# Where the split weights and the activations start in on-chip memory: weights at 256 past a multiple of 512 bytes, activations at multiples of 512

## What is computed

```
layer 0: h += attention(rmsnorm(h))      # 8 heads over 9 chunks of 64 frames, 8 heads over 2 chunks
         h += (silu(n @ w_gate) * (n @ w_up)) @ w_down        # n = rmsnorm(h), inner width 2816
layer 1: h += (u * spatial_mix(rmsnorm(v))) @ w_out           # u, v = gelu(n @ w_in)
         h += top-2-of-8 experts, each a gate/up/down network  # inner width 3584
out = rmsnorm(h)
```

## Time and profile before

| | us |
|---|---|
| median of three executions | 3757.09 |
| lowest, highest | 3750.78, 3783.22 |
| the profiled execution, its own time | 3749.22 |
| its span, first to last instruction | 3747.5 |
| PE busy | 3575.2 (95%) |
| PEld busy | 3458.3 (92%) |
| DVE busy | 1760.1 (47%) |
| ACT busy | 1660.6 (44%) |
| mean granted TensorE clock | 0.981 of full speed |

### The profile page before, as it was taken

How to read it: one execution, slowest core, us unless ns; L and a number is a source line. 1 busy time by engine, 2 the same in 40 slices (tenths; PEclk the granted TensorE clock), 3 DMA queues, 4 the chain that set the end, 5 groups by cost and what they waited for, 6 DMA issues and landing times.

```text
span 3747.5 us, 76188 instructions
## 1 busy us (share of the span) xinstructions
PE 3575.2 (95%) x29176; PEld 3458.3 (92%) x29176; DVE 1760.1 (47%) x2508; ACT 1660.6 (44%) x2316; POOL 106.9 (3%) x137
## 2 busy tenths in 40 slices
PE   8999899999999999959999999999999999999993
PEld 5888799999999899659999999999999999999993
DVE  4455543333333544435555555554554444544444
ACT  3455433323332332236465564554654544544542
POOL 1000000000000000020000000000000000000001
PEclk9999999999999999979999999999999999999997
DMA  5111322333333422176666666556564455554446
GB/s 178 35 49 43 131 95 90 95 93 121 96 95 96 134 63 69 40 187 194 209 194 196 206 193 210 182 188 201 190 206 155 164 178 165 166 177 159 158 154 236
DMA packets 154482, 542.59 MB, mean 145 GB/s; under 512 B 18312, under 2 KB 18352, under 8 KB 154368
## 3 DMA queue, kind: packets, MB, share of 16 engines
q1 hardware_dynamic: 128592, 468.25, 39.2%
q0 software_dynamic: 16496, 55.52, 4.2%
q10 hardware_dynamic: 9280, 17.24, 1.6%
HBM read 511.31 MB, written 33.28 MB: 145 GB/s over the span
## 4 chain that ended last, share of the span: by engine, by line
PE 93%; DVE 2%; DMA 2%; ACT 1%; issue 1%; POOL 0%; ACTq 0%; POOLq 0%; DVEq 0%
PE ps L292 87%; PE ps L341 1%; PE ps L580 1%; PE ps L565 1%; PE ps L519 1%; DMA y<-yrow_d,slot 1%; PE ps L1524 1%; PE ps L1553 0%; PE ps L588 0%; PE ps L600 0%; DMA tok_d<-tokid,slot 0%; PE ps L1320 0%; PE ps L543 0%; ACT eA L639 0%; DVE wl L279 0%
## 5 line engine op out<-in xcount | busy, mean ns | idle before, releaser
L279 DVE TENSOR_TENSOR wl<-wraw,wh 128x1024 fp32r<-128x1024 f32 x876 | 1072.1, 1225 | 1462.1 <-ACT wh L275 1461.9
L275 ACT ACTIVATE wh<-wraw 128x1024 fp32r<-128x1024 f32 x876 | 921.4, 1058 | 1023.6 <-PE ps L292 1014.9
L292 PE MATMUL ps<-exh,wh 128*128 128x240 f32 (+3 forms) x3584 | 1021.0, 285 | 12.5 <-issue 10.1
L292 PE MATMUL ps<-exl,wh 128*128 128x240 f32 (+3 forms) x3584 | 1020.2, 285 | 0.0
L292 PE MATMUL ps<-exh,wl 128*128 128x240 f32 (+3 forms) x3584 | 1019.9, 285 | 0.0
L292 PE MATMUL ps<-xs,wh 128*128 128x256 f32 x5248 | 828.1, 280 | 3.1 <-DVE qAl L626 2.0
L292 PEld LDWEIGHTS ps<-xs,wh 128*128 128x128 f32 x5248 | 703.9, 189 | 11.6 <-issue 7.6
L292 PEld LDWEIGHTS ps<-exh,wh 128*128 128x128 f32 x3584 | 678.5, 189 | 13.4 <-issue 13.4
L292 PEld LDWEIGHTS ps<-exl,wh 128*128 128x128 f32 x3584 | 676.6, 189 | 0.0
L292 PEld LDWEIGHTS ps<-exh,wl 128*128 128x128 f32 x3584 | 676.6, 189 | 0.0
L292 PE MATMUL ps<-xs,wl 128*128 128x256 f32 x2624 | 518.1, 279 | 0.0
(11 more groups left out here) (280 smaller groups left out, 2802.6 us busy)
## 6 DMA issues: line engine op xcount, KB each, us to landing
wraw<-in_w_expert SPq DMA_DIRECT2D x676, 512.0 KB, 3.6
wraw<-in_w_main SPq DMA_DIRECT2D x200, 512.0 KB, 3.6
yrow_d<-yst ACTq DMA_DIRECT2D x16, 512.0 KB
yT<-in_xT POOLq DMA_DIRECT2D x4, 1024.0 KB, 10.3
hT<-in_xT POOLq DMA_DIRECT2D x2, 2048.0 KB, 10.0
h_d<-hT POOLq DMA_DIRECT2D x2, 2048.0 KB, 10.0
hT<-h_d POOLq DMA_DIRECT2D x2, 2048.0 KB, 13.6
xrow_d<-rows ACTq DMA_DIRECT2D x16, 256.0 KB, 2.0
```

The source lines that it names most:

```text
L275: act.activation(wh[:, j], wraw[:, j], ACT.Copy).then_inc(hi_done, 1)
L279: dve.tensor_tensor(wl[:, j], wraw[:, j], wh[:, j].bitcast(F32), ALU.subtract).then_inc(lo_done, 1)
L292: mm = pe.matmul(out[:, s], a, b[:, s], start=first and part == 0 and c == 0, stop=last and part == 2 and c + w == n)
```

## The change

No instruction, loop, semaphore or DMA is added, taken away or moved: on each of the five engines the order of instructions is the same. Only tensors are declared in another order. `gains` goes ahead of the weights and pushes them up by 128 bytes. `itab`, `nitem` and `upto` go to the end of the layout, behind `acc`, where they lie over nothing that is in use with them. A 64-byte tensor that nobody reads, `to_512`, fills the place before the activations.

```diff
+        gains = sb("gains", [P, 4, KD])
         wraw = sb("wraw", [P, 4, 1024])
         wh = sb("wh", [P, 4, 1024], F32R)
         wl = sb("wl", [P, 4, 1024], F32R)
         ident = sb("ident", [P, P])
         ones = sb("ones", [P, P])
-        gains = sb("gains", [P, 4, KD])
         epsc = sb("epsc", [P, 1])
...
         tokl = sb("tokl", [P, CAP // P], U32)
-        itab = sb("itab", [1, 3, NCAND + 1], I32)
-        nitem = sb("nitem", [1, 1], I32)
-        upto = sb("upto", [1, len(WIDTHS) + 1], I32)
+        sb("to_512", [P, 16])
...
         acc = sb("acc", [P, HALF], F32, s2)
+        itab = sb("itab", [1, 3, NCAND + 1], I32, s2)
+        nitem = sb("nitem", [1, 1], I32, s2)
+        upto = sb("upto", [1, len(WIDTHS) + 1], I32, s2)
         s2.close()
```

## The result

The changed kernel took 3795.58 us, the median of four executions (3794.92 to 3797.17). Beside it the kernel before took 3757.99, also of four (3750.78 to 3783.22). The ratio on record is 1.009 (that of the two medians is 1.010), with a 95% interval of 1.005 to 1.0129: slower by about one per cent. The profiled execution took 3797.17 us, its span is 3795.6, which is 48.1 us more than before. In the changed file `product`'s matmuls are line L293, and every later line is one further down.

A forecast was written before the change was run, and what follows sets the result against it. PE was taken to bound the kernel, through the three matmuls of `product` (L292). All terms were taken as 0 on the profiled 3749.2 us; with the median at 3757.1, the forecast was 3753 us, range 3630 to 3870.

The forecast's parts named there:

- weights and activations 256 apart instead of 192: Some 26,100 matmuls of L292, in the dense network and experts: new operand distance forecast to cost 0 us.
- best end: L292's products: all that is paid above the bound goes, together 196 us less, 3553 us left.
- worst end: L292's products: every one pays the value projections' 19.5 ns above its streaming time, 237 us more, 3986 us.
- the 109 ns: Pace of weight loads, read from twelve transposes of L1553 in 1.31 us; the bound for 240 and 256 columns.
- DVE, ACT and the transposes: Weight splitting covered by at least 2.7 us of PE work a unit, transposes at the weight-load pace; 0 us.
- The three transfers on the chain: DMA writes to moved tensors, 35.8 us on the chain; a tenth either way is 4 us, taken as 0.
- the lock: Phase of two streams at their start: 256-column matmuls share two paces anew, -31 to +32 us, taken as 0.
- A: L292's products: addresses count for nothing, or the change misses what matters; 3753 us, from 3715 to 3787; chance 0.44.
- B: L292's products: half of 512 bytes apart is better; 3651 us, from 3553 to 3715; chance 0.34.
- C: Experts and dense network: slower, excess half way between 192 and 320 apart; 118 us more, 3867 us; chance 0.22.
- the likeliest case: Whole kernel: addresses count for nothing, own range 3715 to 3787 us; chance 0.44.

The follow-up runs named there:

- its two twins: Two other layouts at distance 0 modulo 256: one pad of 64 bytes before the activations, or both operands starting at 320; 3800.14 and 3797.1 us.

## Why the prediction was wrong

**The step that failed** is the one on "weights and activations 256 apart instead of 192": "I take 0, since the only variation that the trace shows in one and the same product happens with no address changed". The distance decides the pace of these products. At a distance of 0 modulo 256 the 256-column matmuls cost 4.6 ns more than the mean of before. With the weights left where they were and the activations moved by one pad of 64 bytes to that distance, the loss is the same (`same_apart_256`).

**Why the reason given was none.** I argued that the pieces of a unit walk through all starts modulo 4096 and the pace does not move. They walk in steps of 512, and the activations in steps of 1024, 1536 or 2048. All of these are multiples of 256, the period that the runs showed. The trace of before had one distance in it, 192 modulo 256, for activations moving. It could not speak about another. Constancy over the variations that happen to be in a trace was taken for constancy over all.

**What was right.** The best end and worst end held: no product left them. Something is paid above the 109 ns and the columns' time, and it is the product's own. DVE, ACT and the transposes cost nothing more, as taken. The three transfers on the chain took 35.1 us instead of 35.8, which one trace of each cannot tell from chance. The facts behind the lock were read rightly: at the distance 192 two paces stand side by side with 256 columns (and two or three at 32, 128, 160 and 208), each trace changes between them only across a break in the stream, and which of them is taken changes from kernel to kernel. That a phase of the two streams "certainly" sets it is more than any run showed. The two paces fit the spread of the kernel before: its executions lie up to 30 us apart (3739.93 to 3769.97 in one set of 19), about the 31 or 32 us that I gave the lock either way. The four of the changed kernel, with one pace, lie within 2.3. But its two twins, with the same pace, spread over 9 and 10 us, and only the profiled executions show their paces, so this is an argument.

**A reading that stood on too little.** I called 109 ns the pace of the weight loads, from twelve float32 transposes of 128 columns. By my own reading of L1320, float32 takes two passes, and two passes of 128 columns are 107 ns by themselves. The trace of before has a better row, which I did not use: L292's 64 matmuls `ps<-wsl,vgh`, in the reduced format with 128 columns. They start 111 ns apart (median from their starts), far above the 53 ns of their columns. The bound was about right, then, but not from the row that I gave.

**The rivals.** A was the forecast and fell: it wanted 883 or 849 in 100 us, and 834 came. B fell for 256 columns and held, by little, for 288 and 304: those went faster by 1.6 and 1.0 ns. C named the right place and came within 1 ns for 256 columns (5.4 said, 4.6 measured). That closeness is luck: its way there, half way from 192 to 320, was wrong, because 320 behaves as 64 does. Its 3867 us was 71 us too high, since it made all widths dearer. The time lay inside the range of 3630 to 3870, though outside the 3715 to 3787 of the likeliest case, and the forecast was no change.

**The rule of the Trainium skill** ("TensorE: Matmul & The Clock Gate", Part 2) is that loading the next weights takes no read bandwidth from the running matmul. I had drawn from it that an address could change nothing. The runs do not agree with that: with the same instructions, 256 columns took from 113.3 to 123.3 ns in layouts that differ only in where tensors start. Whether it is read bandwidth that is lost, no run shows.

**What stays open.** That the two reads meet in some part of the memory with a period of 256 bytes is an argument, not a reading. No run took the weight load away from beside the matmul. The order of the prices over the widths (208 has the fastest pace with 288 columns and the slowest with 256) has no explanation here. Neither has what picks one of several paces after a break.

## What to carry to other kernels

When TensorE streams one operand of such products while it loads the other, treat the distance between their starts, modulo 256 bytes here, as a tuning value of its own: try several, and read the pace for each width from the count of matmuls in a steady stretch. Do it for the widths that hold most of the matmuls; the best distance for one is not the best for another, and a separate pad for each stage lets each have its own. Take several executions, since one layout can have more than one pace. A constant pace in a trace says nothing about a variation that the trace does not contain.

## What the runs showed of the hardware

- The pace of these matmuls, each with a weight load, depends on the distance of the operands modulo 256 bytes and, at the multiples of 64 where starts were varied, not on the starts: 120.0 ns with 256 columns at 0, at 256, and at 256 with other starts; 118.7 at 128 and 384, but for some 800 matmuls of the one and 300 of the other at 120.0; 117.8 at 64 and, but for some 700 of its matmuls, at 320.
- A step of 16 bytes can matter: 288 columns take 133.3 ns at 192, 131.1 at 208, 133.3 at 224.
- At one distance (192) there are two stable paces for 256 columns, 113.3 and 117.8 ns, each held over more than a thousand matmuls and changed only across a break in the stream. Other distances have several too: 117.3, 118.7 and 120.0 ns at 160; 117.8, 118.3 and 123.3 at 208.
- At distance 0 one weight load for 512 columns instead of two for 256 each saves 13.3 ns, 60 us in the whole kernel (3735.3 against 3795.6 us).
